# A modulation step cut by feature, with the first norm and the first projection pair run block by block between its parts

## What is computed

```python
mod_x = (silu_c @ w_ada[i] + b_ada[i])[:, None, :]
mod_c = (silu_cc @ w_ada[i] + b_ada[i])[:, None, :]
sh1, sc1, g1, sh2, sc2, g2 = jnp.split(mod_x, N_MOD, axis=-1)
csh1, csc1, cg1, csh2, csc2, cg2 = jnp.split(mod_c, N_MOD, axis=-1)

hx = modulate(rms_norm(x, norm1_g[i]), sh1, sc1)
hc = modulate(rms_norm(ctx, norm1_g[i]), csh1, csc1)
qx, kx, vx, ux = split_proj(hx @ w_in[i])
```

## Time and profile before

| | us |
|---|---|
| runs | 2696.69, 2692.78, 2683.35 |
| median | 2692.78 |
| profiled execution, its own time | 2692.5 |
| its span, first to last instruction | 2690.4 |
| TensorE busy in it | 2532.0 (94%) |
| VectorE / ScalarE / GpSimd busy | 1314.0 / 755.1 / 865.7 |
| first projection matmul starts | 55.98 |
| first pair of units ends | 81.12 |

### The profile page before, as it was taken

The page is one execution under the profiler, slowest core; times in us unless marked ns, Lnnn a source line. Parts: engine busy times, 40 slices in busy tenths (PEclk is TensorE's granted clock), DMA queues, the critical chain, the costliest instruction groups (busy, mean ns, idle before and its releaser), DMA issues.

```text
span 2690.4 us, 33826 instructions
## 1 busy us (share of the span) xinstructions
PE 2532.0 (94%) x13640; PEld 2062.0 (77%) x13640; DVE 1314.0 (49%) x1303; ACT 755.1 (28%) x1140; POOL 865.7 (32%) x380
## 2 busy tenths in 40 slices
PE   5999888897999999999989989999999999999999
PEld 3788677586887878878767678888888877777877
DVE  4799688535444444444484767841023221343131
ACT  4201277504121111211244367731000110241010
POOL 1343300033444435344423200024444434514332
PEclk8999899998999999999989999999999999999999
DMA  6111465210111111111121100001111111202112
GB/s 252 40 40 55 123 178 179 98 47 32 47 54 41 55 40 55 47 48 47 48 94 40 32 1 1 1 32 47 62 48 55 48 40 55 64 31 110 47 40 86
DMA packets 54841, 165.64 MB, mean 62 GB/s; under 512 B 5348, under 2 KB 23912, under 8 KB 53288
## 3 DMA queue, kind: packets, MB, share of 16 engines
q1 hardware_dynamic: 49008, 140.68, 16.2%
q10 hardware_dynamic: 5688, 22.81, 2.2%
HBM read 152.98 MB, written 10.49 MB: 61 GB/s over the span
## 4 chain that ended last, share of the span: by engine, by line
PE 84%; DVE 8%; ACT 3%; issue 2%; DMA 2%; POOL 1%; SPq 0%; ACTq 0%; DVEq 0%; POOLq 0%
PE region L272 24%; PE region L274 24%; PE region L273 24%; PE pv L1546 2%; PE aux L1536 2%; PE pv L349 1%; DVE conv L1031 1%; ACT na_prob L921 1%; DVE tmp L425 1%; PE aux L358 1%; PE pv L887 1%; DVE h_lo L419 1%; DMA rs_again<-rs_spill 1%; DVE x L1844 1%; DVE na_prob L962 1%
## 5 line engine op out<-in xcount | busy, mean ns | idle before, releaser
L1924 POOL TENSOR_TENSOR w_hi<-w_raw,der 128x1024 fp32r<-128x1024 f32 x186 | 362.0, 1946 | 1787.7 <-PE region L274 1742.2
L272 PE MATMUL region<-h_hi,w_hi 128*128 128x512 f32 x1760 | 693.7, 394 | 43.7 <-DVE h_lo L419 20.7
L274 PE MATMUL region<-h_hi,w_lo 128*128 128x512 f32 x1760 | 689.6, 392 | 0.0
L273 PE MATMUL region<-h_lo,w_hi 128*128 128x512 f32 x1760 | 689.5, 392 | 0.0
L1927 POOL TENSOR_TENSOR w_lo<-w_raw,w_hi 128x1024 fp32r<-128x1024 f32 x186 | 503.1, 2705 | 14.6
L272 PEld LDWEIGHTS region<-h_hi,w_hi 128*128 128x128 f32 x1760 | 333.6, 190 | 114.7 <-issue 41.0
L273 PEld LDWEIGHTS region<-h_lo,w_hi 128*128 128x128 f32 x1760 | 333.7, 190 | 76.2 <-issue 8.0
L274 PEld LDWEIGHTS region<-h_hi,w_lo 128*128 128x128 f32 x1760 | 333.1, 189 | 70.4
L272 PE MATMUL region<-ff_hi,w_hi 128*128 128x512 f32 x512 | 199.2, 389 | 0.0
L273 PE MATMUL region<-ff_lo,w_hi 128*128 128x512 f32 x512 | 199.2, 389 | 0.0
L274 PE MATMUL region<-ff_hi,w_lo 128*128 128x512 f32 x512 | 199.2, 389 | 0.0
(11 more groups left out here) (332 smaller groups left out, 3858.7 us busy)
## 6 DMA issues: line engine op xcount, KB each, us to landing
w_raw<-units SPq DMA_DIRECT2D x186, 512.0 KB, 3.5
w_raw<-w_ada_late SPq DMA_DIRECT2D x32, 512.0 KB, 4.3
bias<-na_bias SPq DMA_DIRECT2D x24, 384.0 KB, 3.8
ada_buf<-w_ada SPq DMA_DIRECT2D x4, 2048.0 KB, 13.5
x_sb<-x_t ACTq DMA_DIRECT2D x2, 2048.0 KB, 13.7
v_pair<-v_spill SPq DMA_DIRECT2D x64, 64.0 KB, 3.3
x<-x_t ACTq DMA_DIRECT2D x1, 4096.0 KB, 13.5
x_spill<-x ACTq DMA_DIRECT2D x1, 4096.0 KB, 11.4
```

What stands on the lines that cost most here:

```text
L272: pe.matmul(dst, wh, xh, start=first, stop=False)
L273: pe.matmul(dst, wh, xl, start=False, stop=False)
L274: return pe.matmul(dst, wl, xh, start=False, stop=last)
L1924: pool.tensor_tensor(w_hi[:, s], w_raw[:, s], one_col.broadcast_to([P, 1024]), ALU.mult)\
```

## The change

- **Weights by feature.** The host lays `w_ada` out so that group g holds the shift and the scale of feature blocks 2g and 2g+1. With group g done, blocks 2g and 2g+1 can be scaled.
- **Four buffers.** `ada_buf` becomes four tiles, so SP issues all groups without a wait; the two weight units stand between groups 1 and 2.
- **Sums packed.** `first_sums_pe` sums each quarter of the tokens into a group of 32 partitions of `aux` (four 32x256 matmuls a block). Root and reciprocal work on 128x256, and a new `spread` (four matmuls of 256 columns) writes the inverse root to all partitions of `aux`, from which DVE multiplies.
- **Order.** PE: sums, group 0, spread, turn 0, group 1, turn 1, group 2, blocks 0 and 1 of both units, turn 2, group 3, blocks 2 and 3, turn 3, blocks 4 to 7. The two units of the pair go block by block together instead of three blocks apart. DVE makes bias and gain of a group right after its turn (`ada_mod_dve`): groups 0 and 1 ahead of block 0, group 2 ahead of block 4's multiply, group 3 ahead of block 6's. ACT copies the rows of groups 2 and 3 after blocks 0 and 2.
- **PSUM.** The group results go to `pv` and no longer to `region`, so the pair starts as the first use of `region`.
- **Names.** The attention semaphores of both layers are shared, with counts offset; their instructions and order stay.

```diff
     "rms": [("r1", 8), ("rc", 8), ("rm", 8)],
...
-    "att": [("ma", 32)],
+    "att": [("na", 0), ("mla", 0), ("ma", 0)],
...
-    ada_buf = place("ada_buf", [2, KD, HALF], 0)
+    ada_buf = [place(f"ada_buf{g}", [KD, HALF], at) for g, at in enumerate([128, 144, 0, 16])]
...
-    def ada_sp(e, pos):
-        for g in range(N_ADA):
-            if g >= 2:
-                reach(e, "ada_mm", 4 * (g - 1))
-            e.dma_start(ada_buf[:, g % 2], w_ada[g]).then_inc(sem(f"ada_ld{g % 2}"), 16)
+    def ada_sp(e, g):
+        e.dma_start(ada_buf[g][:], w_ada[g]).then_inc(sem(f"ada_ld{g}"), 16)
+
+    def ada_pe(e, g):
+        reach(e, f"ada_ld{g}", 16)
+        if g:
+            reach(e, "ada_row", g)
+        for k in range(KD):
+            quarter = slice(32 * (k % 4), 32 * (k % 4) + 32)
+            last = e.matmul(pv[quarter, 0, 0:HALF], silu_wide[:, k], ada_buf[g][:, k], start=(k < 4), stop=(k >= 4))
+            if k >= 4:
+                last.then_inc(sem("ada_mm"), 1)
...
+    def ada_mod_dve(e, ch, g):
+        reach(e, "ada_tr", g + 1)
...
+        e.tensor_tensor(made, turned, bias, ALU.add).then_inc(sem("ada_mod"), 1)
+        reach(e, "ada_mod", g + 1)
...
+    def first_norm_dve(e, ch):
+        def low(k):
+            reach(e, "n1_hi", k + 1)
+            e.tensor_tensor(h_lo[:, k], tmp[:, k % 2], h_hi[:, k].bitcast(F32), ALU.subtract).then_inc(sem("n1_lo"), 1)
+
+        inverse_dve(e, "r1", 1, tmp[:, 3, 0:QTR])
+        ada_mod_dve(e, ch, 0)
+        ada_mod_dve(e, ch, 1)
+        reach(e, "r1_spread", 1)
+        for k in range(KD):
+            if k >= 2:
+                reach(e, "n1_lo", k - 1)
+            e.tensor_tensor(tmp[:, k % 2], x_sb[:, k], aux[:], ALU.mult).then_inc(sem("n1_nm"), 1)
+            if k:
+                low(k - 1)
+            if k in (3, 5):
+                ada_mod_dve(e, ch, (k + 1) // 2)
...
+        first_sums_pe(e)
+        reach(e, "silu_c", 1)
+        ada_pe(e, 0)
+        reach(e, "r1_rs", 1)
+        spread(e, aux[:], tmp[:, 3, 0:QTR]).then_inc(sem("r1_spread"), 1)
+        ada_turn_pe(e, 0)
+        ada_pe(e, 1)
+        ada_turn_pe(e, 1)
+        ada_pe(e, 2)
+        blocks(0, 2)
+        ada_turn_pe(e, 2)
+        ada_pe(e, 3)
+        blocks(2, 4)
+        ada_turn_pe(e, 3)
+        blocks(4, KD)
+        pos.use += 2
+
+    def first_act(e):
+        root_act(e, "r1", tmp[:, 3, 0:QTR], aux[:, 0:QTR], D, eps_col)
+        ada_row_act(e, 0)
+        ada_row_act(e, 1)
+        first_norm_act(e, 0)
+        ada_row_act(e, 2)
+        first_norm_act(e, 1)
+        first_norm_act(e, 2)
+        ada_row_act(e, 3)
+        for k in range(3, KD):
+            first_norm_act(e, k)
```

More of the change, by code:

```diff
@@ L388, in rms_act @@
         reach(e, f"{tag}_sqmm", nk)
-        root_act(e, tag, tmp[:, rs, 0:width], aux[:, 0:width], n, eps_col)
+        if root:
+            root_act(e, tag, tmp[:, rs, 0:width], aux[:, 0:width], n, eps_col)
     def root_act(e, tag, dst, src, n, eps):
@@ new lines, in ada_pe, with ada_turn_pe @@
+    def ada_pe(e, g):
[7 more added lines that the diff above has]
+                last.then_inc(sem("ada_mm"), 1)
+    def ada_turn_pe(e, g):
+        reach(e, "ada_row", g + 1)
+        reach(e, "quad", 1)
+        if g:
+            reach(e, "ada_mod", g)
+        for m in range(4):
+            last = e.matmul(pv[:, 1, 8 * g + 2 * m:8 * g + 2 * m + 2], ada_row[:, g % 2, m * P:(m + 1) * P], quad, start=True, stop=True)
+        last.then_inc(sem("ada_tr"), 1)
@@ new lines, in ada_row_act, with two_streams @@
+    def ada_row_act(e, g):
+        reach(e, "ada_mm", 4 * (g + 1))
+        if g >= 2:
+            reach(e, "ada_tr", g - 1)
+        copy(e, ada_row[:, g % 2], pv[:, 0, 0:HALF]).then_inc(sem("ada_row"), 1)
+    def two_streams(first, n):
+        return der[:, 0:96].rearrange("p (two c) -> p c two", two=2)[:, first:first + n]
+    def ada_mod_dve(e, ch, g):
+        reach(e, "ada_tr", g + 1)
+        made = two_streams(0, 16).rearrange("p (s k) two -> p s k two", s=2)[:, :, 2 * g:2 * g + 2]
+        turned = pv[:, 1, 8 * g:8 * g + 8].rearrange("p (s k two) -> p s k two", s=2, two=2)
+        bias = sp_("b_ada", 16).rearrange("p (s k) -> p s k", s=2)[:, :, 2 * g:2 * g + 2].unsqueeze(3).broadcast_to([P, 2, 2, 2])
+        e.tensor_tensor(made, turned, bias, ALU.add).then_inc(sem("ada_mod"), 1)
+        reach(e, "ada_mod", g + 1)
+        gain = sp_("norm1", 2, 2 * g).unsqueeze(2).broadcast_to([P, 2, 2])
+        ch(e.scalar_tensor_tensor(out=der[:, 64:80].rearrange("p (two k) -> p k two", two=2)[:, 2 * g:2 * g + 2],
+                                  in0=two_streams(8 + 2 * g, 2), scalar=1.0, in1=gain, op0=ALU.add, op1=ALU.mult))
@@ new lines, in first_sums_pe, with first_norm_act @@
+    def first_sums_pe(e):
+        for k in range(KD):
+            reach(e, "r1_sq", k + 1)
+            for q in range(4):
+                last = e.matmul(aux[32 * q:32 * q + 32, 0:QTR], ones[:, 0:32], tmp[:, k % 2, q * QTR:(q + 1) * QTR],
+                                start=(k == 0), stop=(k == KD - 1))
+            last.then_inc(sem("r1_sqmm"), 1)
+    def first_norm_act(e, k):
+        t = tmp[:, k % 2]
+        reach(e, "n1_nm", k + 1)
+        e.activation(t, t, ACT.Identity, scale=a1[:, k:k + 1], bias=mod_x[:, k:k + 1]).then_inc(sem("n1_af"), 1)
+        reach(e, "n1_af", k + 1)
+        copy(e, h_hi[:, k], t).then_inc(sem("n1_hi"), 1)
@@ new lines, in first_norm_dve @@
+    def first_norm_dve(e, ch):
[6 more added lines that the diff above has]
+        reach(e, "r1_spread", 1)
+        for k in range(KD):
+            if k >= 2:
[5 more added lines that the diff above has]
+                ada_mod_dve(e, ch, (k + 1) // 2)
+        low(KD - 1)
+        reach(e, "n1_lo", KD)
@@ new lines, in first_pair_pe, with blocks @@
+    def first_pair_pe(e, pos):
+        assert pos.use % 2 == 0 and UNIT0["u"] % 2 == 0
+        def blocks(a, b):
+            for k in range(a, b):
+                reach(e, "n1_lo", k + 1)
+                w = slice(k * P, k * P + P)
+                for n in range(2):
+                    if k == 0:
+                        e.wait_ge(unit_split, UNIT0["u"] + n + 1)
+                    for lo in (0, HALF):
+                        last = mm3(e, region[:, n, lo:lo + HALF], w_hi[:, n, w], w_lo[:, n, w],
+                                   h_hi[:, k, lo:lo + HALF], h_lo[:, k, lo:lo + HALF], k == 0, k == KD - 1)
+                    if k == KD - 1:
+                        last.then_inc(unit_done, 1)
+        first_sums_pe(e)
[14 more added lines that the diff above has]
+        pos.use += 2
@@ L531, in proj1_pe @@
     def proj1_pe(e, pos):
-        start_pair(e, pos, UNIT0["u"], h_hi, h_lo, lambda k: reach(e, "n1_lo", k + 1))
-        reach(e, "r1_root", 1)
+        first_pair_pe(e, pos)
         rms_pe(e, "rc", KD, CTX)
```

25 lines of the change are left out of this document (12 added, 13 removed).

## The result

| | before | after |
|---|---|---|
| median, us (range) | 2692.72 (2683.35 to 2696.69) | 2671.86 (2668.18 to 2672.06) |
| runs | 4 | 4 |
| span of the profiled execution | 2690.4 | 2670.1 |

The ratio is 0.9919, with a 95% interval of 0.9907 to 0.9931.

A forecast was written before the change was run, and what follows sets the result against it. TensorE bounds nearly the whole span except the first 56 us, a dependence chain. The start gains 13.5 us, 5.3 given back inside the pair: 2692.5 - 8.2 = 2684.3, 2684.5 from the median; range 2677 to 2692.

The forecast's parts named there:

- the end of the pair: End of the first two projection units, used as sole price: 72.9 against 81.1, 8.2 us earlier, reaching the kernel's end.
- Costed at nothing: Effects priced at zero: POOL's later split of unit 2, shifted ctx and rope landings, renamed attention semaphores.
- group 0 / spread: PE after the column sums: first modulation group 1.9 to 3.3 us; inverse-root spread 3.78 at low clock, half at high.
- Start: First projection matmul, before at 55.98, would come at 41.4 or 43.3, taken as 42.5; 45.8 if later.
- Multiply from PSUM: DVE's first-norm multiply, reading its second operand from PSUM, costs 1.23 us even beside POOL, instead of 3.38.
- Small steps beside POOL: DVE's bias and gain steps before the first block, while POOL splits weights: 0.2 plus 1.2 to 1.8 us.
- Group 2: Third modulation load lands by 36, is used up on PE by 38 to 40, and doesn't set the start.
- Inside the pair: First two projection units take 30.4 us instead of 25.1: 24.2 matmuls, 4.0 modulation work, 2.1 waits.
- Warm and short: Opening: high PE clock through block 0 and smaller waits give 12 to 14 us, 2679 to 2681; chance 0.17.
- Late group 2: Queued loads slow each other, third group lands at 44, start 46, gain 4.7 us, 2688; chance 0.06.
- Clock stays low: TensorE stays at 1.2 GHz through the first projection units, ending at 88.9, 7.8 us later: 2700.5; chance 0.05.
- Lost behind: Something after the first projection units ends last anyway, or the change doesn't reach the end: 2692; chance 0.05.

The follow-up runs named there:

- a_head0: The kernel after with TensorE's MLP loop placed at the start of a block of 256 instructions; 2672.10 us, ratio 0.9925 to the kernel before.
- b_head0: The kernel before with only TensorE's MLP loop placed at the start of a block of 256 instructions; 2682.06 us, ratio 0.9957.
- b_pad79: The kernel before with 79 already-met wait instructions added at the head of TensorE's list; 2683.87 us, ratio 0.9963.
- b_sems: The kernel before with only the attention semaphores shared and their counts offset; 2693.73 us, ratio 1.0003.
- a_head224: The kernel after with TensorE's MLP loop placed at instruction 224 of a block, so it spans 8 blocks; 2669.87 us, ratio 0.9908 to before.
- a_head239: The kernel after with TensorE's MLP loop placed at instruction 239 of a block, 17 instructions in its first block; 2674.74 us, ratio 0.9932 to before.
- b_head224: The kernel before with TensorE's MLP loop placed at instruction 224 of a block, so it spans 8 blocks; 2681.69 us, ratio 0.9959.

## Why the prediction was wrong, point by point

**The step that failed** is the one by which everything was priced: "So I price the change by one number, the end of the pair, before 81.1, and assume that a shift of it reaches the end of the kernel." The shift does reach the end (9.87 at the pair's end, 10.17 at 546 us, and a_head0 against b_head0 10.0 in the medians); what was wrong is that it was taken for the whole. But the change has a second effect that no dependence carries: 79 more instructions on TensorE move its MLP loop in the code blocks. It is worth 11.3 us by b_head0, 9.9 by b_pad79; the two traces show 8.0 of it at the three turns (18.45 less 10.50). The sum closes within the scatter: 10.0 + 9.9 to 11.3 is 19.9 to 21.3, measured 20.9. With the loop held in place in both kernels the measured gain is 10.0 where 8.2 was forecast: the opening's mechanism was right and the forecast of it a little small; the other half was not foreseen at all. None of my rivals had it. "Costed at nothing" went through loads, splits and semaphores, not the place of the code, though before's trace has the three waits of 2.4 to 2.8 us with no releaser in a loop whose data were ready.

**The opening**, by the prediction's own terms:

| term | predicted | after |
|---|---|---|
| last square ends | 23.9, back to back | 24.18, with a pause of 0.25 in the last four |
| reciprocal ends | 27.5 | 27.8 |
| group 0 / spread | 1.9 to 3.3 / half of 3.78 | 1.97 / 1.99, both at the high clock |
| first multiply starts | 36.4 or 38.3 | 36.97 |
| group 2 lands | by 36, no wait | 37.24, PE waits 2.92 |
| block 0 starts | 42.5 (41.4 to 43.3) | 41.87 |
| wait ahead of block 3 / block 5 | 1.7 / 0.4 | 1.29 / none |
| the pair | 30.4 | 29.4 |
| pair's end | 72.9 | 71.25 |
| next unit behind it | 7.6 | 7.63 |
| gain of the opening | 8.2 | 9.87 |

- *Start.* Forecast 0.6 us too late: 0.5 of it because the multiply started at 36.97 and 42.5 stands for 37.5, and 0.1 because from multiply to matmul it took 4.9 where 5.0 was taken. The two starts of the prediction also mix the price of the small steps: 34.4 + 0.2 + 1.8 = 36.4, but 36.9 + 0.2 + 1.2 = 38.3.
- *Multiply from PSUM.* Right: 2.35 us for two, 1.2 each. That it is free of GpSimd isn't shown, since the splits were over at 36.92.
- *Small steps beside POOL.* Taken at 1.2 to 1.8, they took 1.70 and 2.26, and 0.17 where POOL is idle (50.42). The rows show more: 30.98 + 1.70 = 32.68 and 34.67 + 2.26 = 36.93, and POOL's instructions end at 32.65 and 36.92. The step ends when POOL's instruction does: its cost is what is left of that instruction. The rows of before say the same: 47.07 + 1.22 = 48.29 and 48.33 + 1.82 = 50.15, where POOL's instructions end at 48.27 and 50.12. So 1.22 and 1.82 were no prices of such a step, and that taking them came out close is luck. (This agrees with the Trainium skill, "SBUF — State Buffer", section "Who interferes with whom": two SBUF inputs contend with a GpSimd instruction that reads SBUF.)
- *Group 2.* The wait of 2.92 us wasn't in the sum and cost nothing, because TensorE was through with it at 40.92 and block 0 was ready at 41.87. The rate was right (421 GB/s, and 4.9 us from group 2's landing at 37.24 to group 3's at 42.14); both landed about 1.2 us later than the sum of the bytes says, and why wasn't followed. The cover was 0.95 us and not the 4 us of the prediction: the group ran at the low clock (3.64 us and not 1.9), behind the wait.
- *Inside the pair.* 1.0 too dear: the waits were 1.29 instead of 2.1, and block 0 took 4.6 us instead of 5.1 (41.87 to 46.50, its last three matmuls at the high level); the rest came out 0.3 dearer.

**Rivals.** *Warm and short*: its clock for block 0 occurred in a_head0 (pair 27.8 us, as priced) and not in after; its total of 12 to 14 us wasn't reached even there, 11.5. *Late group 2*: late by 1.2 us, with 0.95 us of cover left. *Clock stays low*: no, 1.00 from 45.80 on. *Lost behind*: no, the gain arrived.

**What the parts are worth**, by the medians: place of the loop 9.9 to 11.3 us; of the opening's 10.0, the cut by feature and the interleaving 5.1, the packed sums about 2.4 (within the scatter of the times; the traces say 2.7), the rest (2.5) the early requests and what overlaps between the parts, not measured apart.

**Open.** Some 2 to 3 us between 8.0 at the turns and the 9.9 to 11.3 of the medians aren't located; they are within the intervals (8 to 15). Why block 0 meets one clock level or the other wasn't tried.

## What to carry to other kernels

Before calling a difference of 10 us the merit of an edit, compare the two traces stretch by stretch to the end, and look in every loop of the instruction stream for waits with no releaser at its turns and for more packets on the instruction queue. A gain that comes from where the code lies isn't the edit's: 16 idle instructions give it too, and the next edit can take it away, so fix the loop's place by hand, as in a_head0 and b_head0, and compare kernels with it fixed. Where operands are cut so that the first consumer needs only a part, let other work stand between the parts: here it was worth 5 us, because TensorE worked on a modulation group while the norm of the first block was made.

## What the runs showed of the hardware

- A loop of 1579 TensorE instructions in 7 blocks of 256 isn't fetched again after its first pass, and its closing branch takes 0.2 us; in 8 blocks it is fetched again (26 to 27 packets of 16 KB in three turns), and the branch takes 3.3 to 4.0 us (before, b_sems, a_head224, a_head239, b_head224). A turn then costs TensorE 0 to 0.2 us with 32 instructions ahead of the first block boundary, 1.0 with 17, and 2.6 with 16 or fewer.
- A VectorE step of 128x4 elements with two SBUF inputs took 0.17 us alone and 1.70 or 2.26 beside a GpSimd split, ending within 0.03 us of it (after).
- The same opening ran its first projection block at a granted clock of 0.51 in one execution (after) and 1.00 in another (a_head0), worth 1.66 us at the pair's end.
